# The fourth layer's query and key norms: sum of squares moved into the next slot's projection

## The chip, the cores and the metric

The kernel runs on one core of a Trainium2 chip. The time is device microseconds from the start to the end of one launch. TensorE (PE) does the matmuls, VectorE (DVE) and ScalarE (ACT) the elementwise work, GpSimd (POOL) a little of it, and SyncE (SP) issues the weight loads.

## What is computed

Four layers run one after the other over 256 tokens of width 1024, in fp32: two of a first block, two of a second. The change is in the mixer of the last layer, `odd_mixer` of the reference:

```python
for gi, (window, dil) in enumerate(DIL_PATTERNS):          # 3 groups
    cols = w_in[:, gi * 3 * ATT_W:(gi + 1) * 3 * ATT_W]
    proj = (h @ cols).astype(jnp.float32).reshape(B, T, 3, ATT_HEADS, ATT_DH)
    q = rms_norm_2(proj[:, :, 0], q_norm) * (ATT_DH ** -0.5)
    k = rms_norm_2(proj[:, :, 1], k_norm)
    v = proj[:, :, 2]
    o, lse = dilated_band_attention(q, k, v, dil, window // dil, slopes)
...
wts = jax.nn.softmax(jnp.stack(lses), axis=0)
o = jnp.sum(wts[..., None] * jnp.stack(outs), axis=0)
return o.reshape(B, T, ATT_W).astype(h.dtype) @ w_out
```

`rms_norm_2` divides each head's 128 values by the root of their mean square and multiplies by a gain. There are 8 heads of 128 and three groups with different strides. The kernel takes the three groups' logits as one softmax, which is the same thing as the weighted sum above.

## The kernel before

**Slots.** All weights come as slots of 128 x 2048 floats (1 MB), which SP loads into a ring of six. The mixer of the fourth layer has 36 of them: four head pairs `hp`, and in each nine slots `s`: for each of the three groups a query slot, a key slot (`s % 3 < 2`) and a value slot (`s % 3 == 2`). The query and key slots are numbered apart by `q = hp * 6 + s // 3 * 2 + s % 3`, from 0 to 23. Below, a "quartet" is the nine slots of one `hp`, and its slots are slot 0 to slot 8; the quartet with `hp = 2` is the third.

**Units.** The softmax works on units `u`, four to a head pair: two heads by two blocks of 128 queries. An even unit has 3 blocks of keys (384 logits to a query), an odd one 6 (768). The units of head pair `hp - 1` are worked on between the slots of quartet `hp`, so the first quartet (`hp = 0`) has projections alone, and the fifth pass (`hp = 4`) units alone. Below, u0 to u3 are the four units of a pass.

**Each engine has its own program, written out by hand**, and all loop over `hp` and `s` in the same way; semaphores join them. In step `s` of a quartet:

- PE (`odd_mixers`, L1484): `project_split`, 48 matmuls, each 128x128 by 128x256, in two halves `t` of 24 (weights and input are split into a high and a low part, three products each), into bank `at % 2`; then, where there are units, `values_of(u - 1)` and `scores_of(u)` in even steps or `turn(u)` (3 or 6 transposes of the softmax's result) in odd ones; then, for a query or key slot, `mean_square(q)`: one matmul of ones with the squares, 128x512, in plain fp32, into bank 2. It waits for ACT's squares (`sq`).
- ACT (L1021): `attention_high` makes the high part of slot `s + 3` (L773, 128x2048); then it evacuates slot `s`: `qraw` by a copy (L1059) and `qsq` by a square (L1060), or `vtok` (L1065) for a value slot; then `unit_exp` (L1027, in even steps) or `unit_turned` (L1036, L1039), `unit_out` (L1045), and last the root of `q`'s mean square (L1078), which waits for PE's `mean_square`. Exp and Sqrt need different tables, and an ACT_TABLE_LOAD stands where they alternate.
- DVE (L2392): `attention_low` makes the low part of slot `s + 3` (L1844, 128x2048), then in even steps both parts of `softmax` (L1850, L2417, L1847, then after ACT's exp L2424 and L1847), and then `normed_qk(q)`: a reciprocal of 128x512 (L2400) and a multiplication into `qk` (L1850).

In the trace `qraw` is ff_silu, `qsq` is ff_mid, `qrn` is ff_hid, `qk` is proj, and `vtok`, the logits and the softmax's results are work, since they lie in those buffers. All PE's matmuls have the line of their helper, L1158; transposes in `turn` have L1525.

What joins these steps: PE may project into a bank once the slot two before is evacuated (`sq` or `v`); `scores_of(u0)` waits for the quartet's last key (`qk` of `6 * hp + 5`), `turn(u)` for DVE's result (`prob`), `values_of(u)` for ACT's `turned`. ACT waits before it writes `qraw` of `q` for `qk` of `q - 2`.

Of the kernel before, what the change touches and what calls it, by code (L numbers as in the profile page):

```python
# [12 lines left out]
P = 128  # L13
# [4 lines left out]
EPS = 1e-6  # L18
# [149 lines left out]
def build_program(nc, x_in, cond_in, params_in, consts_in, stream_in, out, plan=PLAN):  # L168
# [6 lines left out]
    with ExitStack() as ctx:  # L175
# [354 lines left out]
        def slot_at(n, s):  # L530

            return place[f"in{n}"] + (PE_AT[plan[n]][s] if plan[n].startswith("first") else s)

        def out_bank(n, s):

            return bank(6 if plan[n] == "odd" and s == 3 else s)
# [211 lines left out]
        def _(act):  # L748
# [272 lines left out]
            def odd_mixers(n):  # L1021
                def unit_exp(u):
                    w = ATT_GROUPS * (u % 2 + 1) * P
                    act.wait_ge(*att_vec["neg"].at("neg", u))
                    if u >= 2:
                        act.wait_ge(*att_pe["turned"].at("turned", u - 2))
                    act.activation(prob[:, u % 2, 0:w], logit[:, u % 2, 0:w], ACT.Exp, bias=neg_q[:, u:u + 1],  # L1027
                                   accum_out=sum_q[:, u:u + 1]).then_inc(*att_act["exp"].step("exp"))

                def unit_turned(u):  # L1030
                    blocks = ATT_GROUPS * (u % 2 + 1)
                    act.wait_ge(*att_pe["turned"].at("turned", u))
                    if u >= 2:
                        act.wait_ge(*att_pe["out"].at("out", u - 2))
                    a = min(blocks, 4)
                    last = act.activation(probT[:, u % 2, 0:a, :], bank(4, 0, a * P).rearrange("p (n m) -> p n m", n=a),  # L1036
                                          ACT.Copy)
                    if blocks > 4:
                        last = act.activation(probT[:, u % 2, 4:6, :],  # L1039
                                              bank(5, 0, 2 * P).rearrange("p (n m) -> p n m", n=2), ACT.Copy)  # L1040
                    last.then_inc(*att_act["turned"].step("turned"))

                def unit_out(u):
                    act.wait_ge(*att_pe["out"].at("out", u))
                    act.activation(yT[:, u // 2, u % 2 * P:u % 2 * P + P], bank(3, 0, P), ACT.Copy)\  # L1045
                       .then_inc(*att_act["out"].step("out"))

                for hp in range(5):
                    for s in range(9):
                        if hp * 9 + s + 3 < 36:  # L1050
                            attention_high(n, hp * 9 + s + 3)
                        if hp < 4:
                            at, g, j = place[f"in{n}"] + hp * 9 + s, s // 3, s % 3
                            q = hp * 6 + g * 2 + j
                            act.wait_ge(weights_used, at + 1)
                            if j < 2:
                                if q >= 2:
                                    act.wait_ge(*att_vec["qk"].at("qk", q - 2))
                                act.activation(qraw[:, q % 2, :], bank((hp * 9 + s) % 2), ACT.Copy)  # L1059
                                act.activation(qsq[:, q % 2, :], bank((hp * 9 + s) % 2), ACT.Square)\  # L1060
                                   .then_inc(*att_act["sq"].step("sq"))
                            else:
                                if hp >= 2 and g == 0:
                                    act.wait_ge(*att_pe["out"].at("out", 4 * (hp - 1) - 1))
                                act.activation(vtok[:, hp % 2, g, :, :],  # L1065
                                               bank((hp * 9 + s) % 2).rearrange("p (t d) -> p t d", t=2), ACT.Copy)\
                                   .then_inc(*att_act["v"].step("v"))
                        if hp >= 1 and s < 8:
                            u = 4 * (hp - 1) + s // 2
                            if s % 2 == 0:  # L1070
                                unit_exp(u)
                            else:
                                unit_turned(u)
                        if hp >= 1 and s >= 2 and s % 2 == 0:
                            unit_out(4 * (hp - 1) + s // 2 - 1)
                        if hp < 4 and s % 3 < 2:
                            act.wait_ge(*att_pe["ms"].at("ms", q))
                            act.activation(qrn[:, q % 2, :], bank(2), ACT.Sqrt, bias=EPS, scale=1.0 / P)\  # L1078
                               .then_inc(*att_act["root"].step("root"))

            def feed_forward(n, kind):
                base, first = tiles_before[n], place[f"ffn{n}"]
# [73 lines left out]
        def _(pe):  # L1156
# [327 lines left out]
            def odd_mixers(n):  # L1484
                first = place[f"in{n}"]

                def project_split(s, to, token_major):

                    pe.wait_ge(*att_low_vec.at("w", s))
                    high, low = (w.rearrange("p (k n) -> p k n", k=KD)  # L1490
                                 for w in (att_high[s % 4], ring_r[:, (first + s) % RING, :]))
                    for t in range(2):
                        c = slice(t * P, t * P + P)
                        for k in range(KD):
                            if s == 0 and t == 0:
                                pe.wait_ge(*att_x_vec.at(f"h{k}", 0))
                            for w, x, end in ((high, att_x_high, 0), (high, att_x_low, 1), (low, att_x_high, 2)):
                                a, b = (x[:, k, c], w[:, k, :]) if token_major else (w[:, k, c], x[:, k, :])
                                last = mm(to[:, t * T:t * T + T], a, b, k == 0 and end == 0, k == KD - 1 and end == 2)
                    last.then_inc(weights_used, 1)  # L1500
# [68 lines left out]
                for hp in range(5):  # L1569
                    for s in range(9):  # L1570
                        if hp < 4:
                            at = hp * 9 + s
                            if at >= 2:
# [2 lines left out]
                                    pe.wait_ge(*att_act["v"].at("v", hb * 3 + sb_ // 3))  # L1576
                                else:
                                    pe.wait_ge(*att_act["sq"].at("sq", hb * 6 + sb_ // 3 * 2 + sb_ % 3))
                            project_split(at, bank(at % 2), s % 3 == 2)
                        if hp >= 1:  # L1580
                            u = 4 * (hp - 1)
                            if s % 2 == 0 and s >= 2:
# [2 lines left out]
                                (scores_of if s % 2 == 0 else turn)(u + s // 2)  # L1585
                            if hp == 4 and s < 8:
                                early_out(n, s)
                        if hp < 4 and s % 3 < 2:
                            mean_square(hp * 6 + s // 3 * 2 + s % 3)
                early_out(n, 8)  # L1590
                for u in (14, 15):
                    pe.wait_ge(*att_act["out"].at("out", u))
# [249 lines left out]
        def _(dve):  # L1842
# [549 lines left out]
            def odd_mixers(n):  # L2392
# [36 lines left out]
                for hp in range(5):  # L2429
                    for s in range(9):  # L2430
                        if hp * 9 + s + 3 < 36:
                            attention_low(n, hp * 9 + s + 3)
                        if hp >= 1 and s % 2 == 0 and s < 8:
                            softmax(4 * (hp - 1) + s // 2, 0)
                            softmax(4 * (hp - 1) + s // 2, 1)
                        if hp < 4 and s % 3 < 2:
                            normed_qk(hp * 6 + s // 3 * 2 + s % 3)

            def out_update(n):
                g = mod_columns(n, 2)  # L2440
# [242 lines left out]
```

## Time and profile before

| | |
|---|---|
| median of three runs | 2593.45 us (2589.7 to 2593.66) |
| the profiled execution | 2587.25 us, span 2585.4 us |
| PE busy | 2504.0 us, 97% of the span |
| DVE, ACT, POOL busy | 1773.6, 1199.2, 333.2 us |
| mean granted TensorE clock | 0.988 of full speed |
| chain that ended last | PE 71%, issue 17%, POOL 6%, DVE 3%, ACT 2% |
| stage of the change (36 slots) | about 2054 to 2319 us of the span |

The profile's page is of one execution, taken by the hardware profiler. A line of the timeline gives an instruction's start in us from the start of the span, its duration, the engine, the line, the operation, what it writes and reads, and in brackets the idle time of the engine before it and what ended it. Matmul ends are modelled and overlap the next matmul, so that the time a matmul takes in a stream is read from start to start. A plain fp32 matmul shows as two records (`x2`).

### The profile page before, as it was taken

To read this page: it belongs to the slowest core of one execution; us is meant where nothing else is said; L and a number is where in the kernel's file an instruction comes from. 1 tells how busy PE (TensorE), PEld (TensorE's weight loads), DVE (VectorE), ACT (ScalarE), POOL (GpSimd) and SP (SyncE) were. 2 spreads that over 40 slices of the span, in tenths; PEclk is the share of its full clock that TensorE was granted. 3 is DMA by queue.
4 is the path that set the end of the run, shared out by engine and by line. 5 is a ranking of instruction groups with operands and counts; after the bars stand their busy time and mean duration, and the time that the engine had idled before them with its cause. 6 is when DMAs were issued, how large, how long until landed. Compare 5 with 4: busy or idle time off the path is not lost.

```text
span 2585.4 us, 36960 instructions
## 1 busy us (share of the span) xinstructions
PE 2504.0 (97%) x14304; PEld 2173.7 (84%) x14304; DVE 1773.6 (69%) x1949; ACT 1199.2 (46%) x1273; POOL 333.2 (13%) x97
## 2 busy tenths in 40 slices
PE   5999999999999999999999999899999999999999
PEld 4889998878888888888888888788999889988998
DVE  5832775768888888888888888365289777863122
ACT  3213213117676767676767676322322446653221
POOL 0005541000000000000000000010454100001542
PEclk8989999999999999999999999999999999999999
DMA  9745884767989998999999989230678443332442
GB/s 367 308 162 211 345 321 171 293 244 266 351 333 350 334 348 335 347 335 346 336 346 337 345 338 361 82 130 1 222 310 320 170 144 144 131 131 103 175 168 92
DMA packets 90383, 656.18 MB, mean 254 GB/s; under 512 B 10032, under 2 KB 10288, under 8 KB 10800
## 3 DMA queue, kind: packets, MB, share of 16 engines
q1 hardware_dynamic: 80928, 589.34, 60.8%
q10 hardware_dynamic: 9360, 65.52, 6.3%
q8 instruction: 67, 1.10, 0.2%
q14 instruction: 28, 0.23, 0.0%
HBM read 653.76 MB, written 1.05 MB: 253 GB/s over the span
## 4 chain that ended last, share of the span: by engine, by line
PE 71%; issue 17%; POOL 6%; DVE 3%; ACT 2%; ACTq 0%; DMA 0%; POOLq 0%; DVEq 0%; SPq 0%
PE bank L1158 70%; POOL ring_rounded L732 6%; PE bank L1703 1%; DVE work L1856 1%; DVE rstd L1904 0%; ACT ff_mid L1060 0%; DVE xT L1850 0%; DMA ring<-stream_dram 0%; DVE ring L1856 0%; DVE ring_rounded L1844 0%; ACT ff_silu L1059 0%; ACT work_rounded L773 0%; DVE yT L1850 0%; ACTq L753 0%; POOL work L692 0%
## 5 line engine op out<-in xcount | busy, mean ns | idle before, releaser
L1844 DVE TENSOR_TENSOR ring_rounded<-ring,work_rounded 128x2048 fp32r<-128x2048 f32 x372 | 842.1, 2289 | 143.6 <-ACT work_rounded L907 122.0
L1158 PE MATMUL bank<-work_rounded,proj_rounded 128*128 128x512 f32 x1792 | 614.3, 406 | 0.7 <-DVE proj_rounded L1844 0.3
L907 ACT ACTIVATE work_rounded<-ring 128x2048 fp32r<-128x2048 f32 x224 | 428.4, 1913 | 0.0
L1158 PEld LDWEIGHTS bank<-work_rounded,proj_rounded 128*128 128x128 f32 x1792 | 338.1, 189 | 77.1 <-issue 2.9
L1158 PE MATMUL bank<-ring_rounded,proj_rounded 128*128 128x512 f32 x896 | 354.1, 395 | 0.0
L1158 PE MATMUL bank<-work_rounded,ff_hid_rounded 128*128 128x512 f32 x896 | 302.5, 398 | 1.8 <-DVE ff_hid_rounded L1844 1.8
L1158 PE MATMUL bank<-yT_rounded,ring_rounded 128*128 128x256 f32 x960 | 271.6, 283 | 0.0
L1158 PE MATMUL bank<-hT,ring 128*128 128x256 f32 x1088 | 247.4, 388 | 1.1 <-ACT hT L797 1.1
L1158 PEld LDWEIGHTS bank<-hT,ring 128*128 128x128 f32 x1088 | 211.0, 195 | 37.8 <-issue 8.5
L1158 PE MATMUL bank<-ff_hid,ring 128*128 128x256 f32 x1056 | 232.9, 379 | 0.0
L1158 PEld LDWEIGHTS bank<-ff_hid,ring 128*128 128x128 f32 x1056 | 198.4, 190 | 25.9
L914 ACT ACTIVATE work_rounded<-ring 128x2048 fp32r<-128x2048 f32 x112 | 214.3, 1913 | 0.0
L1158 PEld LDWEIGHTS bank<-work_rounded,ff_hid_rounded 128*128 128x128 f32 x896 | 170.3, 190 | 43.3 <-DVE ring_rounded L1844 2.0
L1158 PEld LDWEIGHTS bank<-ring_rounded,proj_rounded 128*128 128x128 f32 x896 | 170.7, 191 | 37.0
L1158 PEld LDWEIGHTS bank<-yT_rounded,ring_rounded 128*128 128x128 f32 x960 | 184.1, 192 | 0.0
L1158 PE MATMUL bank<-ring_rounded,ff_hid_rounded 128*128 128x512 f32 x448 | 178.4, 398 | 0.0
L705 POOL COPY ff_hid<-proj 128x4 f32<-128x4 f32 (+1 forms) x2 | 0.7, 362 | 1281.2 <-ACT proj L820 1281.1
L732 POOL TENSOR_TENSOR ring_rounded<-ring,proj_rounded 128x2048 fp32r<-128x2048 f32 x30 | 144.7, 4832 | 129.6 <-ACT proj_rounded L1095 129.6
L930 ACT ACTIVATE ff_hid_rounded<-bank 128x256 fp32r<-128x256 f32 x112 | 43.1, 385 | 253.9 <-PE bank L1703 242.5
L732 POOL TENSOR_TENSOR ring_rounded<-ring,work_rounded 128x2048 fp32r<-128x2048 f32 x30 | 144.4, 4826 | 114.4 <-ACT work_rounded L1095 114.4
L1847 DVE TENSOR_SCALAR ff_mid<-bank,params 128x256 f32<-128x256 f32 x44 | 23.9, 543 | 189.5 <-PE bank L1158 189.5
L1158 PE MATMUL bank<-yT_rounded,proj_rounded 128*128 128x256 f32 x480 | 138.2, 288 | 2.7 <-POOL ring_rounded L732 2.7
(286 smaller groups left out, 4294.9 us busy)
## 6 DMA issues: line engine op xcount, KB each, us to landing
ring<-stream_dram SPq DMA_DIRECT2D x561, 1024.0 KB, 4.8
work<-stream_dram ACTq DMA_DIRECT2D x56, 1024.0 KB, 9.3
params<-params_dram ACTq DMA_DIRECT2D x1, 1728.5 KB, 28.8
consts<-consts_dram ACTq DMA_DIRECT2D x1, 1568.0 KB, 37.4
cond<-cond_dram ACTq DMA_DIRECT2D x2, 512.0 KB, 4.0
xT<-x_dram ACTq DMA_DIRECT2D x1, 1024.0 KB, 10.3
out_dram<-xT SPq DMA_DIRECT2D x1, 1024.0 KB, 3.9
consts<-consts_dram ACTq DMA_DIRECT2D x1, 577.0 KB, 32.2
```

Source lines behind the costliest of these rows:

```text
L705: pool.tensor_copy(d[:, j:4, 0:lag], src[:, j:4, 0:lag])
L732: pool.tensor_tensor(ring_r[:, at, :], ring[:, at, :], f32(w_high[r]), ALU.subtract)\
L907: act.activation(up_high[u][half], ring[:, (moe_first + s + half) % RING, :], ACT.Copy)\
L914: act.activation(down_high[u], ring[:, (moe_first + s) % RING, :], ACT.Copy)\
L930: act.activation(ff_hid_r[:, u, :], bank(4 + u, 0, T), ACT.Copy).then_inc(m["hid_t"], 1)
L1158: return pe.matmul(o, lhsT=a, rhs=b, start=start, stop=stop, skip_group_check=True)
L1703: last = pe.transpose(bank(4 + u, j * P, j * P + P), ff_mid[:, u, j * P:j * P + P], const("ident"))
L1844: return dve.tensor_tensor(o, a, b, op)
L1847: return dve.tensor_scalar(o, a, s1, s2, op0, op1)
L1856: last = dve.scalar_tensor_tensor(half, half, 1.0, row, ALU.mult, ALU.mult, accum_out=column(h))
```

## The change

`normed_of(at)` gives the query or key number of the slot at place `at`, or none. On PE `mean_square` of the slot before is put between the two halves `t` of the next slot's projection, on ACT its root comes right after `attention_high` and ahead of the evacuation of the present slot, and on DVE `normed_qk` comes right after `attention_low` and ahead of the softmax. Nothing is computed otherwise.

```diff
--- before.py
+++ after.py
@@ -530,6 +530,11 @@
         def slot_at(n, s):
 
             return place[f"in{n}"] + (PE_AT[plan[n]][s] if plan[n].startswith("first") else s)
+
+        def normed_of(at):
+
+            hp, s = divmod(at, 9)
+            return hp * 6 + s // 3 * 2 + s % 3 if 0 <= hp < 4 and s % 3 < 2 else None
 
         def out_bank(n, s):
 
@@ -1049,6 +1054,11 @@
                     for s in range(9):
                         if hp * 9 + s + 3 < 36:
                             attention_high(n, hp * 9 + s + 3)
+                        q = normed_of(hp * 9 + s - 1)
+                        if q is not None:
+                            act.wait_ge(*att_pe["ms"].at("ms", q))
+                            act.activation(qrn[:, q % 2, :], bank(2), ACT.Sqrt, bias=EPS, scale=1.0 / P)\
+                               .then_inc(*att_act["root"].step("root"))
                         if hp < 4:
                             at, g, j = place[f"in{n}"] + hp * 9 + s, s // 3, s % 3
                             q = hp * 6 + g * 2 + j
@@ -1073,10 +1083,6 @@
                                 unit_turned(u)
                         if hp >= 1 and s >= 2 and s % 2 == 0:
                             unit_out(4 * (hp - 1) + s // 2 - 1)
-                        if hp < 4 and s % 3 < 2:
-                            act.wait_ge(*att_pe["ms"].at("ms", q))
-                            act.activation(qrn[:, q % 2, :], bank(2), ACT.Sqrt, bias=EPS, scale=1.0 / P)\
-                               .then_inc(*att_act["root"].step("root"))
 
             def feed_forward(n, kind):
                 base, first = tiles_before[n], place[f"ffn{n}"]
@@ -1484,13 +1490,15 @@
             def odd_mixers(n):
                 first = place[f"in{n}"]
 
-                def project_split(s, to, token_major):
+                def project_split(s, to, token_major, between):
 
                     pe.wait_ge(*att_low_vec.at("w", s))
                     high, low = (w.rearrange("p (k n) -> p k n", k=KD)
                                  for w in (att_high[s % 4], ring_r[:, (first + s) % RING, :]))
                     for t in range(2):
                         c = slice(t * P, t * P + P)
+                        if t and between is not None:
+                            mean_square(between)
                         for k in range(KD):
                             if s == 0 and t == 0:
                                 pe.wait_ge(*att_x_vec.at(f"h{k}", 0))
@@ -1576,7 +1584,7 @@
                                     pe.wait_ge(*att_act["v"].at("v", hb * 3 + sb_ // 3))
                                 else:
                                     pe.wait_ge(*att_act["sq"].at("sq", hb * 6 + sb_ // 3 * 2 + sb_ % 3))
-                            project_split(at, bank(at % 2), s % 3 == 2)
+                            project_split(at, bank(at % 2), s % 3 == 2, normed_of(at - 1))
                         if hp >= 1:
                             u = 4 * (hp - 1)
                             if s % 2 == 0 and s >= 2:
@@ -1585,8 +1593,6 @@
                                 (scores_of if s % 2 == 0 else turn)(u + s // 2)
                             if hp == 4 and s < 8:
                                 early_out(n, s)
-                        if hp < 4 and s % 3 < 2:
-                            mean_square(hp * 6 + s // 3 * 2 + s % 3)
                 early_out(n, 8)
                 for u in (14, 15):
                     pe.wait_ge(*att_act["out"].at("out", u))
@@ -2430,11 +2436,12 @@
                     for s in range(9):
                         if hp * 9 + s + 3 < 36:
                             attention_low(n, hp * 9 + s + 3)
+                        q = normed_of(hp * 9 + s - 1)
+                        if q is not None:
+                            normed_qk(q)
                         if hp >= 1 and s % 2 == 0 and s < 8:
                             softmax(4 * (hp - 1) + s // 2, 0)
                             softmax(4 * (hp - 1) + s // 2, 1)
-                        if hp < 4 and s % 3 < 2:
-                            normed_qk(hp * 6 + s // 3 * 2 + s % 3)
 
             def out_update(n):
                 g = mod_columns(n, 2)
```

On PE at the first slots (before; hT and h_heads are the input's high and low parts, work and ring the weights'). The matmul of ff_mid and consts is `mean_square(0)`, behind the 48th matmul of slot 0:

```order
L1158 MATMUL bank<-hT_rounded,work_rounded 128x256
L1158 MATMUL bank<-h_heads_rounded,work_rounded 128x256
L1158 MATMUL bank<-hT_rounded,ring_rounded 128x256
L1158 MATMUL bank<-ff_mid,consts 128x512
L1158 MATMUL bank<-hT_rounded,work_rounded 128x256
L1158 MATMUL bank<-h_heads_rounded,work_rounded 128x256
L1158 MATMUL bank<-hT_rounded,ring_rounded 128x256
```

The same matmul in the changed program; it has moved 24 matmuls on, and what stands around it now is the end of slot 1's first half and the start of its second:

```order
L1164 MATMUL bank<-hT_rounded,work_rounded 128x256
L1164 MATMUL bank<-h_heads_rounded,work_rounded 128x256
L1164 MATMUL bank<-hT_rounded,ring_rounded 128x256
L1164 MATMUL bank<-ff_mid,consts 128x512
L1164 MATMUL bank<-hT_rounded,work_rounded 128x256
L1164 MATMUL bank<-h_heads_rounded,work_rounded 128x256
```

On ACT in the third quartet, slots 0 and 1, from the exp of u0 on, before (work_rounded from ring is `attention_high`, ff_hid from bank the root):

```order
L1027 ACT_TABLE_LOAD
L1027 ACTIVATE work<-work 128x384
L1078 ACT_TABLE_LOAD
L1078 ACTIVATE ff_hid<-bank 128x512
L773 ACTIVATE work_rounded<-ring 128x2048
L1059 ACTIVATE ff_silu<-bank 128x512
L1060 ACTIVATE ff_mid<-bank 128x512
L1036 ACTIVATE work<-bank 128x384
L1078 ACTIVATE ff_hid<-bank 128x512
L773 ACTIVATE work_rounded<-ring 128x2048
```

And now; the high part of slot 4 is ahead of the table load and of the root, and both roots have moved past one high part. The number of table loads is the same:

```order
L1032 ACT_TABLE_LOAD
L1032 ACTIVATE work<-work 128x384
L778 ACTIVATE work_rounded<-ring 128x2048
L1060 ACT_TABLE_LOAD
L1060 ACTIVATE ff_hid<-bank 128x512
L1069 ACTIVATE ff_silu<-bank 128x512
L1070 ACTIVATE ff_mid<-bank 128x512
L1041 ACTIVATE work<-bank 128x384
L778 ACTIVATE work_rounded<-ring 128x2048
L1060 ACTIVATE ff_hid<-bank 128x512
```

On DVE in the same quartet, from the end of u0's softmax to the start of u1's, before (ff_hid from ff_hid is the reciprocal, ring_rounded the low part, work from consts and bank the start of a softmax):

```order
L1847 TENSOR_SCALAR work<-work 128x384
L2400 RECIPROCAL ff_hid<-ff_hid 128x512
L1850 SCALAR_TENSOR_TENSOR proj<-ff_silu,work,ff_hid 128x512
L1844 TENSOR_TENSOR ring_rounded<-ring,work_rounded 128x2048
L2400 RECIPROCAL ff_hid<-ff_hid 128x512
L1850 SCALAR_TENSOR_TENSOR proj<-ff_silu,params,ff_hid 128x512
L1844 TENSOR_TENSOR ring_rounded<-ring,work_rounded 128x2048
L1850 SCALAR_TENSOR_TENSOR work<-consts,bank 128x768
```

And now; between the two softmaxes stand the same six instructions in another order, and the last before u1's softmax is the norm of key 1's slot and no longer the low part of slot 5:

```order
L1853 TENSOR_SCALAR work<-work 128x384
L1850 TENSOR_TENSOR ring_rounded<-ring,work_rounded 128x2048
L2406 RECIPROCAL ff_hid<-ff_hid 128x512
L1856 SCALAR_TENSOR_TENSOR proj<-ff_silu,work,ff_hid 128x512
L1850 TENSOR_TENSOR ring_rounded<-ring,work_rounded 128x2048
L2406 RECIPROCAL ff_hid<-ff_hid 128x512
L1856 SCALAR_TENSOR_TENSOR proj<-ff_silu,params,ff_hid 128x512
L1856 SCALAR_TENSOR_TENSOR work<-consts,bank 128x768
```

## Rows read from the trace of the kernel before

**Rows 1.** Waits of PE, 2040 to 2360 us: who waited for whom, us, times, longest

```profile
PE bank L1158 <- ACT ff_mid L1060: 15.1, 18, 1.2
```

**Rows 2.** Third quartet: length, PE, PEld, DVE, ACT, POOL busy, PEclk, DMA, GB/s

```profile
2192.90:2263.10 70.20, 67.37 (x524) 63.28 (x524) 53.74 (x41) 44.86 (x57) 0.00 (x0) 1.00 0.39 136
```

**Rows 3.** Timeline of PE, end of slot 0 and start of slot 1, first quartet

```profile
2057.23 0.28 PE L1158 MATMUL bank<-h_heads_rounded,work_rounded 128*128 128x256 f32 x1
2057.34 0.28 PE L1158 MATMUL bank<-hT_rounded,ring_rounded 128*128 128x256 f32 x1
2058.80 1.12 PE L1158 MATMUL bank<-ff_mid,consts 128*128 128x512 f32 x2 [1.18 <-ACT ff_mid L1060]
...
2059.89 0.28 PE L1158 MATMUL bank<-h_heads_rounded,work_rounded 128*128 128x256 f32 x1
```

**Rows 4.** Timeline of ACT at the same place: the evacuation of slot 0

```profile
2057.66 0.60 ACT L1059 ACTIVATE ff_silu<-bank 128x512 f32<-128x512 f32 x1 [2.25 <-PE bank L1158]
2058.16 0.59 ACT L1060 ACTIVATE ff_mid<-bank 128x512 f32<-128x512 f32 x1
```

**Rows 5.** Timeline of PE, third quartet: the blocks between projections

```profile
2192.72 0.83 PE L1158 MATMUL bank<-proj 128*128 128x128 f32 x6
2194.06 1.13 PE L1158 MATMUL bank<-ff_mid,consts 128*128 128x512 f32 x2 [0.51 <-ACT ff_mid L1060]
...
2200.71 0.49 PE L1525 MATMUL bank<-consts,work 128*128 128x128 f32 x3
2202.05 1.12 PE L1158 MATMUL bank<-ff_mid,consts 128*128 128x512 f32 x2 [0.85 <-ACT ff_mid L1060]
...
2208.75 0.83 PE L1158 MATMUL bank<-work 128*128 128x128 f32 x6
2209.41 1.46 PE L1158 MATMUL bank<-proj 128*128 128x256 f32 x6
2210.52 0.47 PE L1158 MATMUL bank<-hT_rounded,work_rounded 128*128 128x256 f32 x1
...
2216.37 0.82 PE L1525 MATMUL bank<-consts,work 128*128 128x128 f32 x6
2217.71 1.13 PE L1158 MATMUL bank<-ff_mid,consts 128*128 128x512 f32 x2 [0.52 <-ACT ff_mid L1060]
...
2225.67 0.83 PE L1158 MATMUL bank<-proj 128*128 128x128 f32 x6
2226.34 1.02 PE L1158 MATMUL bank<-ff_mid,consts 128*128 128x512 f32 x2
...
2227.32 0.28 PE L1158 MATMUL bank<-work_rounded,h_heads_rounded 128*128 128x256 f32 x1
...
2247.41 0.82 PE L1525 MATMUL bank<-consts,work 128*128 128x128 f32 x6
2249.19 1.13 PE L1158 MATMUL bank<-ff_mid,consts 128*128 128x512 f32 x2 [0.96 <-ACT ff_mid L1060]
```

**Rows 6.** Timeline of ACT, third quartet, slots 0 and 1

```profile
2194.02 1.28 ACT L1027 ACT_TABLE_LOAD   x1
2195.32 0.62 ACT L1027 ACTIVATE work<-work 128x384 f32<-128x384 f32 x1
...
2196.04 1.28 ACT L1078 ACT_TABLE_LOAD   x1
...
2197.83 1.91 ACT L773 ACTIVATE work_rounded<-ring 128x2048 fp32r<-128x2048 f32 x1
```

**Rows 7.** Timeline of DVE, third quartet, slots 2 to 4

```profile
2210.91 0.95 DVE L1850 SCALAR_TENSOR_TENSOR work<-consts,bank 128x768 f32<-128x768 f32 x1 [0.34 <-PE bank L1158]
...
2214.34 0.62 DVE L1847 TENSOR_SCALAR work<-work 128x768 f32<-128x768 f32 x1
...
2220.36 3.35 DVE L2400 RECIPROCAL ff_hid<-ff_hid 128x512 f32<-128x512 f32 x1 [1.96 <-ACT ff_hid L1078]
...
2224.42 2.28 DVE L1844 TENSOR_TENSOR ring_rounded<-ring,work_rounded 128x2048 fp32r<-128x2048 f32 x1
```

## The prediction, made before the changed kernel was run

> **What bounds the kernel now.** I read the page first: PE is the busy engine everywhere, and only one stage is touched. So the question is what PE waits for in that stage, and I asked for the waits of PE there. One entry stands out: 18 times the sum-of-squares matmul stood still for ACT's squares, 15.1 us in all, 1.2 at most [rows 1]. The other entries of that view are small beside it. Then I took the third quartet as one window [rows 2]: in 70.20 us PE is busy 67.37, DVE 53.74, ACT 44.86, the DMA engines at 0.39, and the granted clock is 1.00, its upper level. So PE sets the pace, nobody else is near it on average, and weights arrive easily. Last I read the timelines, from start to start, since matmul ends are modelled.
>
> In the first quartet the last matmul of slot 0 starts at 2057.34, and one such matmul takes 0.12 in a stream (2057.23 to 2057.34, rounded up), so PE could go on at 2057.46. The sum of squares starts at 2058.80 [rows 3]: 1.34 us of standing still, in which ACT copies and squares the bank, 2057.66 to 2058.75 [rows 4]. This happens at each of the six query and key slots. In later quartets softmax work stands between the projection and the sum of squares and hides part of it.
>
> **What goes: the waits.** Moved by 24 matmuls (2.8 us), the sum of squares finds its squares ready: ACT has them 1.1 us after the bank is full, unless it is late itself. The DVE and ACT work is the same in kind and number; only its order differs, and no DMA moves.
>
> First the cost of the matmul where it now stands. Behind an idle PE it takes 2058.80 to 2059.89 less 0.12, so 0.97 [rows 3]; behind other fp32 work without a wait 2226.34 to 2227.32 less 0.12, so 0.86 [rows 5]. In the middle of a projection no row shows it. Low end 0.86, because its columns must stream in any case. High end 1.16: 0.97, and once more the 0.19 by which the first matmul of a projection is longer after fp32 work (0.47 against 0.28 in its row, [rows 5]) for a change of kind that now comes on both sides. I take 0.92, between the two rows in which the same instruction stands.
>
> - First quartet: 6 x (1.34 + 0.97 - 0.92) = 8.3 us less.
> - Second to fourth quartet: four of the six slots wait. Slot 0: scores start at 2192.72 and take 0.67 (as 2225.67 to 2226.34), the sum of squares starts at 2194.06, so 0.67 lost. Slot 1: three transposes from 2200.71, at 0.12 each to 2201.07, then 2202.05, so 0.98. Slot 3: six from 2216.37 to 2217.09, then 2217.71, so 0.62. Slot 7: the same from 2247.41, then 2249.19, so 1.06 [rows 5]. Slots 4 and 6 have more fp32 work in front and do not wait. Together 3.3 us; the matmul itself is 4 x 0.97 + 2 x 0.86 = 5.6 before and 6 x 0.92 = 5.5 after. So 3.4 for each of three quartets, 10.2 us. 6 + 3 x 4 are the 18 waits of [rows 1].
>
> Together 18.5 us less, if nothing new waits.
>
> **What is late next.** The softmax of u1 now stands behind a norm on DVE, and its result must be there when `turn(u1)` comes. Before, it was there at 2214.96 and the transposes began at 2216.37 [rows 5, 7]: 1.4 us to spare. I walk it through on the third quartet's own times. On ACT the exp of u0 is over at 2196.04 (there its next instruction starts); the high part of slot 4 now goes in there, 1.91, to 2197.95 [rows 6]. The root of slot 0 needs the table load 1.28 and 0.6, so it is ready at 2199.8. DVE: low part 2197.95 to 2200.2 (2.25; the row has 2.28 with some overlap), norm 4.06 (2220.36 to 2224.42) to 2204.3, low part to 2206.5, norm to 2210.6, softmax of u1 4.05 (2210.91 to 2214.96) to 2214.6 [rows 7]. PE: u0's scores end at 2193.39; a projection takes 5.7 to 5.85 (2210.52 to 2216.37 is 5.85, of which some 0.15 is the tail of the scores). Slot 1 with its sum of squares to 2200.1, transposes to 2200.4, slot 2 to 2207.1, values 0.66 (2208.75 to 2209.41) and scores 1.11 (2209.41 to 2210.52) to 2208.9, slot 3 to 2214.7 [rows 5]. DVE 2214.6, PE 2214.7: a tie. Between no wait and 1 us; I take 0.2, so 0.6 for three quartets. Who is queued behind that wait on PE: slot 4's projection, so it counts in full.
>
> The other units have more room. u2 also stands behind a norm, but it is an even unit (a shorter softmax), and a sum of squares now lies in the projection before its transposes. u0 and u3 have no norm in their step. High and low parts are made three slots ahead, which hides a late DVE from the projections. ACT's root in slot 1 is due at 2200.2 for DVE and there at 2199.8: covered by 0.4 us only; if it came later, the norm and with it u1 would be late one for one.
>
> In the fifth pass there is no projection in front of the first unit's scores, and these wait for the last key's norm. Its root comes 2.85 + 0.92 + 0.65 = 4.4 us into slot 35, the norm 4.1 later, at 8.5; PE arrives there after 5.7 + 0.92 and twice 0.66 for values, at 7.9. A new wait of 0.6.
>
> The sum: 18.5 - 0.6 - 0.6 = 17.3; I give 17. Against the profiled execution that is 2587.25 - 17 = 2570. That execution lies 6.2 us under the median of the runs, and 2.4 under the fastest of them; since the changed kernel will be timed by runs, I subtract from the median: **2576.5 us**.
>
> **A rule against the change.** Between the exp and the norms ACT changes tables, and the changed order puts two of the changes (exp of u0, root of slot 0) on the chain that ends at `turn(u1)`. The rows show a load of 1.28, and the exp starts at 2195.32, 0.02 after it [rows 6]; the sum goes by that. The Trainium skill, page "ScalarE: Activation LUTs", section "What ACT_TABLE_LOAD costs", gives such a switch about 1.28 us for the load and 1.38 more for a drain, 2.66 in all. By that rule the chain would be about 2.4 us longer in each of three quartets, an estimate from that page, and the saving some 10 us instead of 17. This trace does not agree so far: load and exp stand end to end.
>
> **Rivals.**
>
> 1. *The softmax of u1 comes late.* The tie breaks against PE by 1 to 4 us in each quartet. One way to it: a table switch costs a second load's time, 1.28, that the order of before hid. Then exp ends 1.28 later, the root 2.56 later, at 2202.4, where the low part would be done at 2201.5, so DVE is late by 1.28 + 0.9 = 2.2, in three quartets 6.6. Time 2593.45 - 17.9 + 6.6 = 2582. For it: the margins of 0.1 and 0.4 us. Against: the end-to-end rows. (The skill's rule named above is of this kind.) Chance 0.20.
> 2. *Only the first quartet gains*, because in the others ACT and DVE, chained through exp, table load, root and norm, set the pace once PE is faster. Then 8.3 - 0.6 = 7.7 less, 2586; a little worse, and nothing can be measured. For it: each waits for the other in turn. Against: 53.74 busy of 70.20 on DVE and 44.86 on ACT [rows 2]. Chance 0.11, of which 0.06 still faster by over 0.2%.
> 3. *Slower.* A whole pair of low part and norm (6.3 us) more than in my walk stands in front of u1's softmax, because DVE enters each quartet late (the norm of slot 7 is now in slot 8), and the sum of squares costs its high end, 0.24 more in 6 places, 1.4. That is 7.7 a quartet, 23.1, and 0.6 at the end, less the 18.5: 2593.45 + 5.2 = 2598.7. The gain is gone from 6 us late a quartet on. Against: my walk of slots 4 to 8 leaves DVE idle before the low parts of slots 8 and 10, where it catches up. Chance 0.04.
> 4. *It does not do what it says.* The order of the programs shows the matmul, root and norm moved in every step, so this could only be a wait that is kept elsewhere, as PE's wait for `sq` two slots on. No change. Chance 0.02.
>
> The forecast has 0.63: from 11 us less (sum of squares at 1.16, which takes 24 x 0.24 = 5.8 off) to 19 us less (0.86, no new waits); 2574 to 2583, and 2 more on both sides for the spread of the runs.
>
> **How the numbers follow.** Range 2569 to 2585: the forecast's with rival 1's, 0.83, with room below because single executions lay up to 6 us under the median. Rival 2 and the slower one are left out. A measurement here tells about 0.2%, 5.2 us, from no change. Faster 0.63 + 0.20 + 0.06 = 0.89; within 0.05 + 0.02 = 0.07; slower 0.04.
>
> **What would show it.** Right: no PE wait on ff_mid at all; the sum of squares in the middle of a projection, 0.86 to 0.97 from start to start; query and key slots of the first quartet 1.4 us shorter; a quartet of 66 to 67 us instead of 70.2; `turn` waits on DVE under 1 us; one wait of 0.6 before the scores of the fifth pass. Wrong: `turn` waits for work L1847 of 1 us and more at u1 (rival 1), quartets of 70 (rival 2), slots growing by more than 1 us with the matmul inside (high end), or a gap between table load and exp.

## The result, and the profile after

The changed kernel takes 2568.2 us (median of six runs, 2563.8 to 2572.5), the kernel before, run beside it, 2588.5 us (six runs, 2582.7 to 2593.7). The ratio is 0.9921, its 95% interval 0.9910 to 0.9931: 20.3 us less, between 17.9 and 23.3. I had forecast 17 us less and 2576.5 us, with a range from 2569 to 2585, so faster was right and the time lies 0.8 us under the range. The profiled execution took 2563.78 us, with a span of 2562.0.

The waits of PE in the stage, 2040 to 2340 us of the changed kernel, whole list:

```profile
PE bank L1164 <- DVE h_heads_rounded L1856: 1.4, 6, 0.5
PE bank L1164 <- ACT work L1041: 1.2, 2, 0.6
PE bank L1164 <- DVE proj L1856: 0.7, 1, 0.7
PE bank L1533 <- DVE work L1853: 0.4, 2, 0.2
```

The 15.1 us in 18 waits on the squares [rows 1] are gone altogether. One entry is new: 0.7 us, once, for DVE's norm (proj L1856), the one forecast for the fifth pass. In the third quartet PE shows no idle time, as far as modelled ends can tell (window of one quartet; length, then busy PE, PEld, DVE, ACT, POOL, granted clock, DMA share, GB/s), where it was 67.37 of 70.20 before [rows 2]:

```profile
2175.90:2242.20 66.30, 66.30 (x524) 63.07 (x523) 53.57 (x41) 44.58 (x57) 0.00 (x0) 1.00 0.40 144
```

The sum of squares in its new place, between two halves; first quartet, then third, with the transposes of u1 at the end (timeline of PE):

```profile
2055.65 0.28 PE L1164 MATMUL bank<-hT_rounded,ring_rounded 128*128 128x256 f32 x1
2055.76 1.02 PE L1164 MATMUL bank<-ff_mid,consts 128*128 128x512 f32 x2
...
2056.75 0.28 PE L1164 MATMUL bank<-h_heads_rounded,work_rounded 128*128 128x256 f32 x1
...
2179.09 1.02 PE L1164 MATMUL bank<-ff_mid,consts 128*128 128x512 f32 x2
...
2180.07 0.28 PE L1164 MATMUL bank<-h_heads_rounded,work_rounded 128*128 128x256 f32 x1
...
2197.35 0.88 PE L1533 MATMUL bank<-consts,work 128*128 128x128 f32 x6
```

Between the sum and the next row shown stands one fp32r matmul, which takes 0.12 in a stream. From 2055.76 to 2056.75 less 0.12 is 0.87, from 2179.09 to 2180.07 less 0.12 is 0.86: as much as behind other fp32 work without a wait, and 0.1 less than behind an idle PE [rows 3, 5].

The chain to `turn(u1)` on ACT and DVE in the same quartet:

```profile
2178.81 1.90 ACT L778 ACTIVATE work_rounded<-ring 128x2048 fp32r<-128x2048 f32 x1
2180.72 1.28 ACT L1060 ACT_TABLE_LOAD   x1
2182.02 0.60 ACT L1060 ACTIVATE ff_hid<-bank 128x512 f32<-128x512 f32 x1
```

```profile
2180.74 2.29 DVE L1850 TENSOR_TENSOR ring_rounded<-ring,work_rounded 128x2048 fp32r<-128x2048 f32 x1 [1.18 <-ACT work_rounded L778]
2182.95 3.35 DVE L2406 RECIPROCAL ff_hid<-ff_hid 128x512 f32<-128x512 f32 x1
...
2189.20 3.35 DVE L2406 RECIPROCAL ff_hid<-ff_hid 128x512 f32<-128x512 f32 x1
...
2193.26 0.95 DVE L1856 SCALAR_TENSOR_TENSOR work<-consts,bank 128x768 f32<-128x768 f32 x1
...
2196.67 0.62 DVE L1853 TENSOR_SCALAR work<-work 128x768 f32<-128x768 f32 x1
```

DVE goes from the low part to the end of u1's softmax without a gap, except 1.1 us in which it waits for the exp. The softmax is done at 2197.29 and the transposes start at 2197.35: the tie of the forecast. The table load and the root stand end to end (2180.72 + 1.28, then 2182.02), as before the change.

How long is the stage? I measure from the first evacuation of slot 0 (`qraw`) to the start of the fifth pass's first softmax on DVE. Before, that is from 2057.66 [rows 4] to this row of the chain:

```profile
2327.87 0.57 DVE work L1850
```

270.21 us. Now these are the two ends:

```profile
2053.12 0.60 ACT L1069 ACTIVATE ff_silu<-bank 128x512 f32<-128x512 f32 x1 [2.26 <-PE bank L1164]
```

```profile
2304.42 0.55 DVE L1856 SCALAR_TENSOR_TENSOR work<-consts,bank 128x384 f32<-128x384 f32 x1 [1.03 <-PE bank L1164]
```

251.30 us, so the stage is 18.9 us shorter. From the first evacuation of one quartet to that of the next it was 65.09, 70.17 and 70.17 us, and is 56.35, 66.32 and 66.33. The spans differ by 23.4 us, though: the changed kernel's profile reaches the stage 4.5 us earlier, and nothing is changed up to there. That was the first thing to settle.

### The profile page after: what moved, and what is told of

It is laid out like the page before. It is cut to its first block, busy times and chain, and to the rows that moved or that the text cites. A ratio compares the mean times of both kernels' runs of the same rounds, so it can differ in the third digit from the quotient of the medians.

```text
span 2562.0 us, 36960 instructions
## 1 busy us (share of the span) xinstructions
PE 2496.2 (97%) x14304; PEld 2170.4 (85%) x14304; DVE 1773.8 (69%) x1949; ACT 1199.0 (47%) x1273; POOL 333.2 (13%) x97
## 4 chain that ended last, share of the span: by engine, by line
PE 72%; issue 17%; POOL 6%; DVE 3%; ACT 1%; ACTq 0%; DMA 0%; POOLq 0%; DVEq 0%; SPq 0%
PE bank L1164 71%; POOL ring_rounded L737 6%; PE bank L1709 1%; DVE work L1862 1%; DVE rstd L1910 0%; DVE xT L1856 0%; DMA ring<-stream_dram 0%; DVE ring L1862 0%; PE bank L1533 0%; DVE ring_rounded L1850 0%; DVE yT L1856 0%; ACTq L758 0%; ACT work_rounded L778 0%; POOL work L697 0%; PE bank L1635 0%
```

## Experiments

The stage length is read as above in each profile. It repeats to 0.05 us, where whole runs spread over several us.

| kernel | stage, us | quartets 1, 2, 3 | ratio to before (95%) |
|---|---|---|---|
| before | 270.21 | 65.09, 70.17, 70.17 | |
| before, again | 270.25 | 65.12, 70.16, 70.18 | 0.9998 (0.9989 to 1.0007) |
| changed | 251.30 | 56.35, 66.32, 66.33 | 0.9921 (0.9910 to 0.9931) |
| changed, again | 251.35 | 56.35, 66.37, 66.36 | 0.9926 (0.9912 to 0.9939) |
| PE alone | 253.38 | 56.34, 67.05, 67.00 | 0.9946 (0.9932 to 0.9959) |
| sum twice | 271.97 | 61.64, 71.47, 71.47 | 1.0005 (0.9996 to 1.0014) |
| sum later | 258.27 | 56.41, 67.70, 67.66 | 0.9955 (0.9939 to 0.9970) |
| softmax first | 251.10 | 56.35, 66.27, 66.27 | 0.9917 (0.9900 to 0.9933) |
| last norm in halves | 250.49 | 56.35, 66.32, 66.37 | 0.9922 (0.9905 to 0.9938) |
| ACT's root back | 267.58 | 56.35, 73.19, 71.96 | one run, 2581.7 us |
| DVE's norm back | 265.20 | 56.36, 69.80, 71.74 | one run, 2579.8 us |
| softmax first and halves | 250.30 | 56.35, 66.26, 66.28 | 0.9926 (0.9912 to 0.9939) |
| sum in fp32r | 240.26 | 52.74, 63.86, 63.86 | 0.9880 (0.9865 to 0.9896) |
| all three | 235.95 | 52.73, 62.73, 62.75 | 0.9863 (0.9848 to 0.9878) |

**Before and changed, again** (no edit).

> The kernel before, once more, to see how much two executions of one program differ and where. In the two profiles so far, the one of the changed kernel reaches the first evacuation of the fourth layer's mixer 4.5 us earlier (2053.12 against 2057.66 us), though nothing is changed up to there. Theory 1 (only the stage is changed; the rest is spread between executions): ratio to before 1.000 within 0.001; the first evacuation starts anywhere from 2052 to 2059 us; the stage from that evacuation to the start of the first softmax of the fifth pass is 270.2 us again (2057.66 to 2327.87) within 0.3. Theory 2 (the change gives 4.5 us ahead of its stage too): the first evacuation is at 2057 to 2058 again.

> The changed kernel once more, on the same chip. Theory 1: 18 to 20 us under before (ratio 0.9923 to 0.9930), since the stage from the first evacuation to the first softmax of the fifth pass is 251.3 us again (2053.12 to 2304.42) and so 18.9 us shorter, and all else is equal on average. Theory 2: 23 us under before, with the first evacuation again 4 us or more ahead of that of the kernel before.

The stage repeats (270.25, 251.35), its start does not: 2057.66 and 2055.77 us in the two profiles of before, 2053.12 and 2053.22 in those of the changed kernel, and from 2053.1 to 2060.4 over all fourteen profiles of this study, of programs that are alike up to there. The two profiles of before alone lie 1.9 us apart. To see where it arises, I follow the same DVE instructions through two profiles. The changed kernel's profile is 0.4 us behind at 130 us; it gains 1.7 us on that of before up to 170, 1.7 between 470 and 500, 1.1 between 1550 and 1673, and 0.5 in a slow drift elsewhere, which makes the 4.5. Each of these parts has stretches in which the granted clock differs. The first one before and changed (columns as above, granted clock third from the end):

```profile
140.00:160.00 20.00, 19.53 (x79) 15.46 (x78) 12.57 (x11) 4.10 (x6) 0.00 (x0) 0.84 0.27 105
```

```profile
140.00:160.00 20.00, 18.54 (x80) 14.89 (x80) 13.37 (x13) 4.27 (x6) 0.00 (x0) 0.90 0.31 116
```

From 470 to 490 us it is 0.91 and 1.00. The two profiles of before agree within 0.4 us up to 1000 us; 1.2 of their 1.9 us arise between 1550 and 1673, where before again has the lower clock early (0.83 against 1.00 from 1630 to 1640) and before has it later and longer. Before, then before again:

```profile
1650.00:1660.00 10.00, 9.95 (x39) 8.77 (x40) 3.56 (x14) 6.50 (x13) 0.00 (x0) 0.59 0.00 0
```

```profile
1650.00:1660.00 10.00, 9.65 (x49) 8.10 (x48) 5.21 (x17) 7.76 (x15) 0.00 (x0) 0.83 0.00 0
```

So theory 1 holds for the stage. Theory 2, that the change also moves its start, is not needed: kernels that have the whole change start the stage anywhere from 2053.1 to 2058.4 (last norm in halves, below), and PE alone at 2060.43, the latest of all. With four profiles of the pair, though, a small share of it is not excluded. The second ratio, 0.9926, is 19.1 us of 2587.2.

**PE's part alone.** In the changed kernel, ACT's and DVE's moves undone:

```diff
-q = normed_of(hp * 9 + s - 1)
-if q is not None:
-    act.wait_ge(*att_pe["ms"].at("ms", q))
...
     unit_out(4 * (hp - 1) + s // 2 - 1)
+if hp < 4 and s % 3 < 2:
+    act.wait_ge(*att_pe["ms"].at("ms", q))
...
-q = normed_of(hp * 9 + s - 1)
-if q is not None:
-    normed_qk(q)
...
     softmax(4 * (hp - 1) + s // 2, 1)
+if hp < 4 and s % 3 < 2:
+    normed_qk(hp * 6 + s // 3 * 2 + s % 3)
```

> Only PE's part of the change: the sum of squares between the halves of the next projection. ACT's root and DVE's norm stay where they were in their programs (end of the step). Theory 1 (the gain is PE's own waits; the moves on ACT and DVE only keep the softmax of u1 in time): no PE wait on the squares; first quartet as in the changed kernel (56.4 us); from the second quartet on the low part and the norm in front of u1's softmax come about 1 us later than in the changed kernel, so turn(u1) waits 0 to 1.2 us in each of three quartets; the stage is 251 to 255 us. Theory 3 (the moved root and norm carry part of the gain): quartets 2 to 4 stay above 68 us each, the stage above 259.

```profile
PE bank L1532 <- DVE work L1852: 2.0, 5, 0.5
```

The stage is 253.4: PE's move alone brings 16.8 of 18.9 us. Of the other 2.1 us, 1.6 are small waits of `turn` for the softmax (2.0 in the view, 0.4 in the changed kernel). Theory 3 falls: it had quartets above 68 us, and they are 67.

**The sum twice.**

```diff
+mm(bank(2), const("ones"), qsq[:, q % 2, :])
 mm(bank(2), const("ones"), qsq[:, q % 2, :]).then_inc(*att_pe["ms"].step("ms"))
```

> The changed kernel with the sum of squares computed twice (the second overwrites the first with the same values). It measures what one such matmul costs in the middle of a projection. Theory 1 (PE sets the pace everywhere in the stage and such a matmul costs 0.86 to 0.92): the stage is 20.6 to 22.1 us longer than 251.3. High end of my prediction (1.16 each): 27.8 longer. Rival (ACT and DVE set the pace in quartets 2 to 4): only the first quartet's 6 x 0.9 = 5.4 us and a part of the rest, under 12.

20.6 us longer than 251.35, 0.86 for each of 24, in all quartets alike: (61.64 - 56.35) / 6 = 0.88 in the first, 5.14 / 6 = 0.86 in the others. PE's time counts in full everywhere. The second sum stands behind plain fp32 work and adds 0.86; the first stands between fp32r matmuls and takes 0.86 too, by the timeline above. So neither the entry into plain fp32 nor the way back costs anything that shows.

**The sum later.**

```diff
-if t and between is not None:
-    mean_square(between)
...
 last.then_inc(weights_used, 1)
+if between is not None:
+    mean_square(between)
```

> The changed kernel with the sum of squares behind both halves of the next projection (ahead of the softmax's work) in place of between them, so 2.85 us later; ACT and DVE as in the changed kernel. It measures how much room the chain to turn(u1) has. In the changed kernel's trace the result of u1 is there at 2197.29 and the transposes start at 2197.35. Tie theory (DVE's order is filled from u0's exp to u1's softmax, with about 0.1 us to spare): the norm of slot 1 starts 1.2 us later, so turn(u1) waits 1.1 to 1.3 us in each of three quartets; the fifth pass's wait for the last key grows from 0.7 to about 3.5 us; the stage is 251.3 + 3.5 + 2.8 = 257.6 us. Rival (PE's own waits are all that matters, DVE has room): 251.3 and at most 2.8 at the end, 254.1.

```profile
PE bank L1533 <- DVE work L1853: 3.7, 4, 1.2
PE bank L1164 <- DVE proj L1856: 3.5, 1, 3.5
```

258.3 us, 0.7 off the tie theory's number, with its waits: 1.2 us at `turn(u1)` in each of three quartets and 3.5 in front of the fifth pass. The rival (254.1 at most) falls. So between the halves is early enough, and half a projection later the chain is late; no run has the sum at an earlier place.

**Softmax first on DVE.**

```diff
-q = normed_of(hp * 9 + s - 1)
-if q is not None:
-    normed_qk(q)
 if hp >= 1 and s % 2 == 0 and s < 8:
     softmax(4 * (hp - 1) + s // 2, 0)
     softmax(4 * (hp - 1) + s // 2, 1)
+q = normed_of(hp * 9 + s - 1)
+if q is not None:
+    normed_qk(q)
```

> The changed kernel with DVE's order turned: within a step the softmax comes first and the norm of the slot before after it. PE and ACT as in the changed kernel. Tie theory: u1's softmax starts with its scores, 1.4 us earlier than now, and the norms come later but inside their room, so the stage stays at 251.1 to 251.4 us and the small waits of turn go. Rival (the norm ahead of the softmax is what makes the change work): the norms fall behind, ACT waits to evacuate or the scores wait for the last key, and the stage is 254 us or more.

251.10, as the tie theory has it. The last part of the change, the norm ahead of the softmax, is worth nothing by itself.

**The last norm in two halves**, each with its own semaphore step, and on PE `scores_of(12)` waits for the first and `scores_of(14)` for the second:

```diff
+for h in range(2):
+    c = slice(h * T, h * T + T)
+    dve.reciprocal(qrn[:, q % 2, c], qrn[:, q % 2, c]).then_inc(*last_vec.step(f"rn{h}"))
...
+    done.then_inc(*(att_vec["qk"].step("qk") if h else last_vec.step("half")))
```

> The changed kernel with the last key's norm (number 23) done in two halves of 256 columns, one to a head; the fifth pass's first scores wait only for the first head's half. Theory: the new wait of 0.7 us of PE for DVE's norm at the start of the fifth pass is gone, since the half norm is 2.1 us in place of 4.1; the stage is 250.6 us. Rival (something else would hold these scores): 251.3.

250.49: the 0.7 us wait is gone, and 0.8 of stage with it.

**ACT's root back** at the end of its step, and, in another kernel, **DVE's norm back** (the edits of PE alone, one at a time).

> PE and DVE as in the changed kernel, but ACT's root back at the end of its step, ahead of the next high part. Then the high part of slot 4 waits for the sum of squares of slot 0, and starts 1.7 us later (2180.5 against 2178.8), the low part and both norms on DVE follow, and so does u1's softmax. Tie theory: turn(u1) waits about 1.7 us in each of three quartets, the stage is about 256 us. Rival (ACT's order costs nothing, as ACT is idle a third of the time): 251.3.

> PE and ACT as in the changed kernel, but DVE's norm back at the end of its step, ahead of the next low part. DVE then stands idle from the end of u0's softmax (2179.55) until the root of slot 0 (2182.62), because the low part of slot 4, which filled that time, is queued behind the norm. Chain theory (what counts is what is queued behind what on DVE between u0's exp and u1's softmax): u1's result comes at about 2199.2, turn(u1) waits 1.9 us in each of three quartets, the stage is about 257 us. Rival (only ACT's order matters): 251 to 252.

Both directions held and both sizes were missed: 267.6 in place of 256, and 265.2 in place of 257. Done alone, each of the two undoings costs 14 to 16 us; together (PE alone, above) they cost 2. The waits of PE, with ACT's root back and then with DVE's norm back:

```profile
PE bank L1532 <- DVE work L1852: 10.0, 7, 2.5
PE bank L1163 <- DVE proj L1855: 2.3, 4, 0.7
```

```profile
PE bank L1533 <- DVE work L1853: 9.8, 6, 3.4
```

DVE in the third quartet, with ACT's root back (start of the low part of slot 4), and with DVE's norm back (start of u0's softmax, then the norm of slot 0):

```profile
2192.78 2.29 DVE L1849 TENSOR_TENSOR ring_rounded<-ring,work_rounded 128x2048 fp32r<-128x2048 f32 x1 [3.10 <-ACT work_rounded L778]
```

```profile
2184.08 0.55 DVE L1856 SCALAR_TENSOR_TENSOR work<-consts,bank 128x384 f32<-128x384 f32 x1
...
2189.90 3.35 DVE L2406 RECIPROCAL ff_hid<-ff_hid 128x512 f32<-128x512 f32 x1 [3.09 <-ACT ff_hid L1060]
```

With one side moved only, high part, table load and root stand in a row on ACT (the high part last when the root is back, first when the norm is back), and DVE waits for the end of the row, 3.1 us, before it has anything to do; in the changed kernel it waits 1.18 and makes the low part while ACT loads the table. And the delay does not end with the quartet, which my expectations had left out: with the norm back, u0's softmax starts at 2184.08 although its scores had started on PE at 2181.20, because DVE was still at two low parts (2179.68 to 2184.08) behind the last norm of the quartet before. In the changed kernel, and with both sides moved back (PE alone), DVE has run empty by then and waits for the scores, so nothing is carried over:

```profile
2176.46 0.56 DVE L1856 SCALAR_TENSOR_TENSOR work<-consts,bank 128x384 f32<-128x384 f32 x1 [1.45 <-PE bank L1164]
```

```profile
2184.49 0.55 DVE L1855 SCALAR_TENSOR_TENSOR work<-consts,bank 128x384 f32<-128x384 f32 x1 [1.24 <-PE bank L1163]
```

Waits are not the whole of it. The granted clock is 1.00 all through the stage in every kernel of the table but these two. With the norm back it falls to its lower level, 0.50, twice, each time behind a wait of 3.4 us of PE for u1's softmax, here in the third quartet (timeline of PE, then a window):

```profile
2206.50 0.88 PE L1533 MATMUL bank<-consts,work 128*128 128x128 f32 x6 [3.39 <-DVE work L1853]
```

```profile
2208.00:2211.00 3.00, 3.00 (x16) 3.00 (x16) 1.89 (x1) 3.00 (x5) 0.00 (x0) 0.50 0.00 0
```

The fp32r matmuls start 0.21 apart there, in place of 0.12, from 2207.96 to 2211.17. That makes some 1.5 us for each fall (an estimate from these rows). With ACT's root back it falls once, in the second quartet, behind the first of three waits of 2.5 us, and not behind the other two. So of the 13.9 us with the norm back, 9.7 are waits in PE's list beyond those of the changed kernel and some 3 the clock; of the 16.3 us with the root back, 11.7 and some 1.5. The remainders, 1 and 3 us, were not taken apart. In the sum later the clock falls too, behind the wait of 3.5 us, but after the end of what I call the stage, so that the 258.3 us do not hold it.

**The sum in fp32r, and all three.** In the changed kernel `qsq` and ones get tiles of the type fp32r, so that the sum is one of rounded squares; the last kernel has this, softmax first and the last norm in halves together.

```diff
-mm(bank(2), const("ones"), qsq[:, q % 2, :])
+mm(bank(2), ones_r, qsq[:, q % 2, :])
```

> The two helpful changes together in plain fp32: softmax ahead of the norm on DVE, and the last key's norm in two halves. They touch different places, so they add: the stage is 251.1 - 0.8 = 250.3 us. Rival: they share a wait, 250.5 or more.

> The changed kernel with the sum of squares as one fp32r matmul: ACT writes the squares rounded to fp32r, and ones are copied once into an fp32r tile. So the norm's sum is of rounded squares. Doubling the sum showed that PE pays 0.86 us for each in full; an fp32r matmul of 512 columns should cost about a quarter (an estimate: the plain one shows as two records and takes 0.86 for 512 columns, the fp32r ones 0.12 for 256). Theory: 0.64 less for each of 24; the first quartet 3.9 us shorter (52.5); in the others PE has 3.9 less too, but the tie at turn(u1) breaks, as PE comes 1.3 us earlier and DVE does not: 63.6 a quartet, with waits of turn of about 1.2 us in each; the stage about 239 us. Rival (DVE and ACT now set the pace): quartets of 65 us and more.

> All three together: the sum of squares in fp32r, softmax ahead of the norm on DVE, the last norm in halves. With the softmax first the chain to turn(u1) is 1.4 us shorter, so the tie holds: quartets of 62.5 us, the stage 250.3 - 24 x 0.64 = 234.9 us, up to 237 if the norms, pushed behind the softmax, make ACT or the scores wait. Against the kernel before that is 35 us less, ratio about 0.9865. Rival: 239 as without the two others.

Softmax first and halves together give 250.30, which is 251.35 less 0.25 and 0.8, so they add. In fp32r the sum takes 0.23 (2058.25 to 2058.48 in the kernel with all three):

```profile
2058.25 0.39 PE L1170 MATMUL bank<-h_heads_rounded 128*128 128x512 f32 x1
2058.48 0.28 PE L1170 MATMUL bank<-hT_rounded,work_rounded 128*128 128x256 f32 x1
```

Alone it brings 11.1 us (240.3 where I had 239; the matmul takes 0.23 and not 0.21, and between 250.30 and 235.95, the two kernels without waits of `turn` for u1, lie 0.60 a sum and not 0.64), with waits of `turn` of up to 1.1 us, since PE now comes earlier and DVE does not; with the softmax first these go (63.86 to 62.73 a quartet), so here the order on DVE that was worth nothing in plain fp32 is worth 1.1 us a quartet. All three reach a stage of 235.95 us, and 2550.7 us where before takes 2586.8: 34.3 us less by the stage, 36 by the medians, ratio 0.9863 (0.9848 to 0.9878), the fastest of this study and faster than both kernels.

## Why the prediction was right, and where it was off

**Right.** The mechanism: PE stood still for the squares, it does not any more, and nobody else takes over. The first quartet is 8.7 us shorter (8.3 forecast), the second and third 3.85 each (3.4 less 0.2 forecast), the fourth with the entry into the fifth pass 2.5 (3.4 less 0.2 and 0.6). The new wait in front of the fifth pass is 0.7 (0.6 forecast). The tie at `turn(u1)` is a tie: from the high part of slot 4 to the end of the softmax 18.5 us, where my walk had 18.6. Rivals 1 and 2 did not come, nor the doubled table switch: load and root stand 0.02 apart, and wherever ACT does not wait for another engine behind a load (15 of 26 between 2050 and 2330 us), its next instruction starts 0.01 to 0.02 after the load. In this trace that part of the Trainium skill's rule (page "ScalarE: Activation LUTs", "What ACT_TABLE_LOAD costs"), the drain on top of the load, does not show.

**The step that failed: what I subtracted from.** The sum was made against the profiled execution, 2587.25 us, and would have given 2570. I then subtracted from the median of three runs, 2593.45, because the changed kernel would be timed by runs. But 6.2 us between two readings of one program was not a property of the profiled execution; the three runs were high. Later medians of before are 2588.5 (the six of the result, these three among them), 2587.2, 2588.6 and 2586.8 us. That step put 5.0 of the 8.3 us of error in (2593.45 against 2588.49).

**Two terms mis-sized, in one direction.** The sum of squares in the middle of a projection costs 0.86, not 0.92: I had taken a value between that behind fp32 work and that behind an idle PE, but a change between fp32r and plain fp32 costs nothing the timeline shows. That is 24 x 0.06 = 1.4 us. And `turn(u1)` costs 0.05, by what softmax first gives back in a quartet, not 0.2: 0.4 us. With both, 17.3 becomes 19.1; the stage measured 18.9. The remaining 1.4 us between 18.9 and the 20.3 of the medians lie inside the interval (17.9 to 23.3). These, the 1.6 us between 17.3 and 18.9, and the 0.3 lost in giving 17 for 17.3 are the other 3.3 of the 8.3 us.

**The range** had 2 us on each side for the spread of runs, while its centre was 5 us off for the same cause. Taken from 2588.5, the forecast of 17 less would have been 2571.5, and 2568.2 inside a range of the same width. Rival 3's mechanism (DVE enters each quartet late) exists: it is what the two kernels with only one side moved back run into. In the changed kernel its condition is not met, since DVE is idle for 1.45 us before u0's softmax in each of the three quartets.

**Open.** Single executions differ by several us before the stage, and the differences arise where the granted clock differs. Why it falls in one execution and not in another at the same place is not shown by any run here.

## What to carry to other kernels

When the busiest engine waits for a short chain through another engine after each step, put the small dependent instruction half a step into the next step's work; the whole wait comes back if the chains behind it have room, and those have to be walked through instruction by instruction, since undoing the move on one side engine alone gave 14 to 16 of 19 us back. Look at the length of the stage in two profiles before trusting a median of a few runs: it repeated to 0.05 us where whole executions spread over 10. And where an engine is shown to be the pace (one instruction doubled costs its full time), make that instruction cheaper next.

## What the runs showed of the hardware

- A change between fp32r and plain fp32 matmuls costs nothing that shows: 0.86 us for a plain 128x512 in the middle of fp32r matmuls, the same as behind plain ones. An fp32r matmul of that size in the same place takes 0.23.
- A wait costs more than its idle time: behind an idle PE the same matmul takes 0.97 to the next one's start [rows 3], 0.11 more than in a stream.
- The same program, up to the same instruction, takes 2053 to 2060 us, and the differences arise in parts where the granted clock differs (0.84 and 0.90 from 140 to 160 us, 0.59 and 0.83 from 1650 to 1660); after that, a stage of 251 us in which the clock is 1.00 repeats within 0.05 us.
- Behind two waits of 3.4 us of PE the granted clock fell to 0.50 for about 3 us, and behind one of 3.5; of three waits of 2.5 us one was followed by such a fall. At 0.50 an fp32r matmul of 256 columns takes 0.21 in place of 0.12.
- Behind 15 table loads nothing shows but the load, 1.28 us.
